# Expert weights in 8 KB runs, with the SSD and routing work in another order, attention scores from high and low parts, and scatters without empty places

## The reference, cut to what matters

```python
h = rms_norm(x, norm_mix)
proj = h @ w_in
# A: attention, 8 heads of 64, causal, with a decay; q and k normalised
sc = einsum('bhqd,bhkd->bhqk', qi, kh) + ci[..., None] - c[:, :, None, :]
# B: GLA, 4 heads, chunks of 64.  C: SSD (Mamba-2), 8 heads, chunks of 64:
y = y_intra + einsum('bhctn,bhcnp->bhctp', cc * exp(acs)[..., None], prev)
y = rms_norm((y + d_skip * xs) * silu(z), out_norm)
x = x + sum(gates * (branches @ w_branch)) @ w_out
t = rms_norm(x, norm_ffn)
# best of 4 groups, then 2 of its 4 experts: 1024 pairs of a token and an expert
for e in range(16):
    hid = silu(t @ w_gate[e]) * (t @ w_up[e])           # 1024 -> 512
    out = out + combine[:, e:e + 1] * (hid @ w_down[e])  # 512 -> 1024
x = x + out
```

## Time and profile before

| | |
|---|---|
| median of three runs | 872.98 us |
| the profiled execution, own time | 872.24 us |
| its span, first to last instruction | 870.5 us |
| mean granted TensorE clock | 0.993 |
| busy: PE, DVE, ACT, POOL | 840.0 (97%), 579.1 (67%), 475.7 (55%), 92.2 us (11%) |
| matmuls on PE | 4188 |
| DMA | 164.26 MB, 189 GB/s over the span |

### The profile page before, as it was taken

One profiled execution on the slowest core, in us unless ns is written; L12 is line 12 of the kernel. 1 busy time (PEld: TensorE's weight loads), 2 busy tenths in 40 slices (PEclk: granted clock), 3 DMA queues, 4 the chain that ended last, 5 costly groups with the idle time before them and its releaser, 6 DMA issues.

```text
span 870.5 us, 11553 instructions
## 1 busy us (share of the span) xinstructions
PE 840.0 (97%) x4188; PEld 673.5 (77%) x4188; DVE 579.1 (67%) x678; ACT 475.7 (55%) x563; POOL 92.2 (11%) x131
## 2 busy tenths in 40 slices
PE   5999999999999989999999999989999999999994
PEld 4777777777877768888888888867888888888883
DVE  5555436766745887324254265788898988889893
ACT  6375445554455242322332332557888788888882
POOL 6510000000000110100000010103112111111001
PEclk9999999999999999999999999999999999999998
DMA  6432012213112031332232494599999999999973
GB/s 213 146 98 72 25 49 98 98 48 98 50 49 97 1 96 49 100 104 97 90 104 97 185 321 164 204 383 347 386 388 369 362 371 377 374 366 352 376 295 49
DMA packets 60173, 164.26 MB, mean 189 GB/s; under 512 B 9592, under 2 KB 10705, under 8 KB 60130
## 3 DMA queue, kind: packets, MB, share of 16 engines
q1 hardware_dynamic: 51504, 145.89, 45.5%
q0 software_dynamic: 4464, 12.66, 6.4%
q10 hardware_dynamic: 4162, 5.13, 1.7%
HBM read 154.16 MB, written 13.11 MB: 192 GB/s over the span
## 4 chain that ended last, share of the span: by engine, by line
PE 90%; DVE 4%; ACT 2%; DMA 1%; issue 1%; POOL 0%; POOLq 0%; DVEq 0%; ACTq 0%
PE bank L1986 26%; PE bank L1988 25%; PE bank L1987 25%; PE bank L2457 1%; PE bank L2108 1%; PE bank L2139 1%; PE bank L2124 1%; DMA xg<-h2rows,tabid 1%; PE bank L2464 1%; PE bank L2096 1%; PE bank L2240 1%; PE bank L2324 1%; PE bank L2190 1%; PE bank L2198 0%; ACT whi L715 0%
## 5 line engine op out<-in xcount | busy, mean ns | idle before, releaser
L737 DVE TENSOR_TENSOR wlo<-mstage,whi 128x2048 fp32r<-128x2048 f32 x95 | 215.5, 2290 | 28.9 <-ACT whi L715 28.8
L715 ACT ACTIVATE whi<-mstage 128x2048 fp32r<-128x2048 f32 x96 | 183.8, 1919 | 25.6 <-PE bank L1988 25.1
L737 DVE TENSOR_TENSOR wlo<-stage,whi 128x2048 fp32r<-128x2048 f32 (+1 forms) x39 | 87.8, 2251 | 96.1 <-ACT whi L715 95.4
L1986 PE MATMUL bank<-hTh,whi 128*128 128x512 f32 x368 | 149.4, 406 | 0.3 <-DVE wlo L1445 0.3
L1988 PE MATMUL bank<-hTh,wlo 128*128 128x512 f32 x368 | 143.7, 390 | 0.0
L1987 PE MATMUL bank<-hTl,whi 128*128 128x512 f32 x368 | 143.4, 390 | 0.0
L715 ACT ACTIVATE whi<-stage 128x2048 fp32r<-128x2048 f32 (+1 forms) x39 | 73.0, 1874 | 75.9 <-PE bank L1988 71.1
L1986 PE MATMUL bank<-whi,xTh 128*128 128x512 f32 (+1 forms) x264 | 104.3, 395 | 2.1 <-DVE xTl L1809 1.1
L1988 PE MATMUL bank<-whi,xTl 128*128 128x512 f32 (+1 forms) x264 | 101.5, 384 | 0.0
L1987 PE MATMUL bank<-wlo,xTh 128*128 128x512 f32 (+1 forms) x264 | 101.2, 383 | 0.0
L1986 PEld LDWEIGHTS bank<-hTh,whi 128*128 128x128 f32 x368 | 69.2, 188 | 17.4 <-issue 2.8
(11 more groups left out here) (383 smaller groups left out, 1333.6 us busy)
## 6 DMA issues: line engine op xcount, KB each, us to landing
mstage<-in_w_exp_gate SPq DMA_DIRECT2D x32, 1024.0 KB, 11.9
mstage<-in_w_exp_up SPq DMA_DIRECT2D x32, 1024.0 KB, 12.0
mstage<-in_w_exp_down SPq DMA_DIRECT2D x32, 1024.0 KB, 12.4
stage<-in_w_in SPq DMA_DIRECT2D x28, 1024.0 KB, 5.0
stage<-in_w_branch SPq DMA_DIRECT2D x6, 1024.0 KB, 5.0
stage<-in_w_out SPq DMA_DIRECT2D x4, 1024.0 KB, 5.1
xin<-in_x SPq DMA_DIRECT2D x4, 512.0 KB, 5.3
x<-in_x SPq DMA_DIRECT2D x4, 512.0 KB, 7.4
```

The costliest lines, as they stand in the source:

```text
L715: nc.scalar.activation(whi_of(u)[:, :, 0:n], source_of(u)[:, :, 0:n], ACT.Copy).then_inc(hi_ready, 1)
L737: nc.vector.tensor_tensor(wlo_of(u)[:, :, 0:n], source_of(u)[:, :, 0:n], whi_of(u)[:, :, 0:n].bitcast(F32), ALU.subtract).then_inc(lo_read ...
L1986: t.matmul(out, lhs[0], rhs[0], start=start, stop=False)
```

## The change

1. **Start.** DVE scales tile 0 too, in the order square 0, scale 0, square 1, scale 1, scale 2, scale 3, and only then copies the parameter columns. PE transposes tile 3 last, after the parameter rows.
2. **Scores.** `foxq` and `foxk` are split into high parts (ACT, 8 copies of 128x512) and low parts (DVE, 8 subtractions). A score is three fp32r matmuls for each head instead of one in float32.
3. **GLA.** One piece of projection is moved ahead of `gout 0`, behind `gprep 1`.
4. **SSD.** DVE updates the state ahead of the output rows, whose work is now an item of its own, `ssdY`. The `lo` items go later.
5. **Routing.** The rows of padding behind the output are gone, and the DMA that cleared them. `normed` makes four operations of 128x256 of every fourth column, instead of two of 128x512 of every second. DVE takes splits of weights and the permutation's low parts in another order. `table()` also makes `tabh`, ids of half rows.
6. **Experts.** Each partition gets one run of 8 KB from a unit of weights, where it got two of 4 KB. So it holds four rows next to each other of gate and up, and two of down; `hid_rows` therefore takes every second column of `hid` as the operand of the transpose. The wait for the load four units before is gone.
7. **Scatters.** Empty places are skipped by a bounds check. The last item has two scatters, each of half rows, which start when their half of `yrow` is there.

```diff
@@ schedule()
-    out += [("gprep", 1), ("gout", 0), ("gmul", 0)]
+    out += [("gprep", 1)]
+    fill(1, last)
+    out += [("gout", 0), ("gmul", 0)]
     lows()
-    fill(5, last)
+    fill(4, last)
...
         out.append(("ssdB", i))
-        lows()
         if i:
             out.append(("ssdC", i - 1))
+        out.append(("ssdY", i))
+        if i == 0:
+            lows()
         fill(3, gates)
         if i + 1 < NT:
             out.append(("ssdA", i + 1))
         out.append(("ssdN", i))
         if i == 0:
             out.append(("gmul", 1))
-        lows()
+        elif low:
+            out.append(low.pop(0))
...
@@ SP, load(u)
-                if not ovf and u >= U_MOE + 4:
-
-                    sp.wait_ge(mstaged[(u - 4 - U_MOE) % 12], after(m, 16, 16 * ((u - 4 - U_MOE) // 12 + 1)))
-                sp.dma_start(mstage[k][:, :, :].rearrange("p (g r) n -> p g (r n)", r=2), src).then_inc(mstaged[k], 16)
+                sp.dma_start(mstage[k][:, :, :].rearrange("p c n -> p (c n)"), src).then_inc(mstaged[k], 16)
...
-                    return w[e, kh * 512:(kh + 1) * 512, :].rearrange("(g p r) n -> p g (r n)", p=P, r=2)
+                    return w[e, kh * 512:(kh + 1) * 512, :].rearrange("(p r) n -> p (r n)", r=4)
...
-                    return w_exp_down[e, fh * 256:(fh + 1) * 256, :].rearrange("(j p) n -> p j n", p=P)
+                    return w_exp_down[e, fh * 256:(fh + 1) * 256, :].rearrange("(p j) n -> p (j n)", j=2)
...
@@ POOL, scatter(i, par)
-                                     compute_op=ALU.add).then_inc(added, 16)
+                                     bounds_check=T - 1, oob_is_err=False, compute_op=ALU.add).then_inc(added, 16)
...
-                scatter(i, i % 2)
+                if i < NEXP - 1:
+                    scatter(i, i % 2)
+            for half in range(2):
+                pool.wait_ge(free[2 + half], B0[2 + half] + NEXP)
+                g.indirect_dma_start(acc.rearrange("t (h c) -> (t h) c", h=2),
+                                     bass.IndirectOffsetOnAxis(tabh[:, half:half + 1], 0),
+                                     yrow[:, 1, half * 512:half * 512 + 512], None, bounds_check=2 * T - 1,
+                                     oob_is_err=False, compute_op=ALU.add).then_inc(added, 16)
...
@@ ACT, start
-            act.wait_ge(rst_done, 1)
-            a.activation(xn[:, 0, :], xin[:, 0, :], ACT.Copy, scale=rst[:, 0:1]).then_inc(xna_done, 1)
...
@@ DVE, normed(i)
-                for r in range(2):
+                for r in range(4):
...
@@ PE, score
-                    for hh, r in enumerate(rows_of):
-                        t.matmul(bank[4 + hh][:, 0:w], foxq[r, pr, i * P:(i + 1) * P], foxk[r, pr, 0:w],
-                                 start=True, stop=False)
+                    for a, b, first in ((foxqh, foxkh, True), (foxqh, foxkl, False), (foxql, foxkh, False)):
+                        for hh, r in enumerate(rows_of):
+                            t.matmul(bank[4 + hh][:, 0:w], a[r, pr, i * P:(i + 1) * P], b[r, pr, 0:w],
+                                     start=first, stop=False)
...
@@ PE, transposes of hid
-                    ins = t.transpose(bank[6][:, j * P:(j + 1) * P], hid[:, j * P:(j + 1) * P], ident[:, :])
+                    ins = t.transpose(bank[6][:, j * P:(j + 1) * P], hid_rows(j), ident[:, :])
```

More of the change, by code:

```diff
@@ L94, in schedule @@
              (0, 1, 3): [("cumh",)], (1, 0, 3): [("tokrows",)], (2, 0, 1): [("bcum",)]}
+    for q in range(4):
+        early.setdefault((1, 1, q), []).append(("parts", q))
     waiting = [[], []]
@@ L137, in schedule @@
         out += exps[1] + taken[half:]
+        if n < 3:
+            out.append(("parts", 5 + n))
         if nxt is not None:
@@ L1083, in _ @@
                     step(a.activation(lge[:, :, :], lge[:, :, :], ACT.Ln, bias=1.0), lnv_done, 2)
+                elif kind == "parts":
+                    m = it[1]
+                    act.wait_ge(qn_done, m + 1)
+                    step(a.activation((foxqh if m < 4 else foxkh)[:, m % 4, :], (foxq if m < 4 else foxk)[:, m % 4, :],
+                                      ACT.Copy), qh_done, m + 1)
                 elif kind == "cumh":
@@ L1663, in _ @@
                     step(v.tensor_tensor(yd, yd, whole(4), ALU.add), free[4], n)
-                    if i:
-                        n = turn(6, ("ye", i)) + 1
-                        dve.wait_ge(full[6], n)
-                        step(v.tensor_tensor(heads(xdt[:, :]), heads(whole(6)), per_head(eacs[:, i, :]), ALU.mult), free[6], n)
-                        step(v.tensor_tensor(yd, yd, xdt[:, :], ALU.add))
-                    step(v.scalar_tensor_tensor(out=yd, in0=yd, scalar=0.5, in1=zs[:, i, :],
-                                                op0=ALU.mult, op1=ALU.mult), sd_y, i + 1)
                     if i == 0:
@@ L1684, in _ @@
                                  *((free[5], n) if q else ()))
+                elif kind == "ssdY":
+                    i = it[1]
+                    yd = ysd[i % 2][:, :]
+                    if i:
+                        n = turn(6, ("ye", i)) + 1
+                        dve.wait_ge(full[6], n)
+                        step(v.tensor_tensor(heads(xdt[:, :]), heads(whole(6)), per_head(eacs[:, i, :]), ALU.mult), free[6], n)
+                        step(v.tensor_tensor(yd, yd, xdt[:, :], ALU.add))
+                    step(v.scalar_tensor_tensor(out=yd, in0=yd, scalar=0.5, in1=zs[:, i, :],
+                                                op0=ALU.mult, op1=ALU.mult), sd_y, i + 1)
                 elif kind == "ssdN":
@@ L1865, in _, with gated @@
                                  pf[:, :, 0, :].unsqueeze(3), ALU.subtract))
-            split_lo(dve, U_MOE + 2)
+            def gated(n, m=None, per=2):
+                dve.wait_ge(full[1], after(m, per, B0[1] + n + 1))
+                dve.wait_ge(free[0], after(m, per, B0[0] + n + 1))
+                v.tensor_tensor(hid[:, :], act1[:, :], whole(1), ALU.mult).then_inc(free[1], 1)
+            split_lo(dve, U_MOE + 4)
+            split_lo(dve, U_MOE + 5)
+            gated(0)
             dve.wait_ge(r_exp, 1)
@@ L1902, in table @@
                 step(v.tensor_copy(tabid[:, :].unsqueeze(2), slots[:, 0:ITEMS, 0:1]), tab_done, 1)
+                for half in range(2):
+                    step(v.tensor_scalar(tabh[:, half:half + 1], slots[:, NEXP - 1, 0:1], 2.0, float(half), ALU.mult,
+                                         ALU.add))
                 step(v.tensor_reduce(tabw[:, :], slots[:, 0:ITEMS, 1:3], AX, ALU.add), tab_done, 2)
```

110 lines of the change are left out of this document (55 added, 55 removed).

## The result

The change makes the kernel slower: 874.77 us (873.88 to 877.12, 14 runs) against 872.89 (871.88 to 873.59, 14 runs), ratio 1.0028, 95% interval 1.0021 to 1.0035. Forecast were 865.0 us and a range to 869.5. The profiled execution has an own time of 873.92 us and a span of 872.2.

A forecast was written before the change was run, and what follows sets the result against it. PE was taken to bound the kernel, with DVE the bound in routing and the DMA engines close behind. The terms summed to -7.6 us on the profiled 872.24, giving 865.0 us on the median, range 861.5 to 869.5.

The forecast's parts named there:

- SSD term: SSD block 1: the state comes earlier, so PE's 3.26 us wait and the clock loss behind it go; -4.4 us.
- Rival (a): SSD: the wait is only exchanged, delayed splits are late for PE, half the term gone; 867.5 us, chance 0.16.
- Clock: SSD: the half clock behind PE's old wait goes, a gain of 1.4 us, between 1.0 and 1.6.
- Scores: Attention scores: three fp32r passes replace a float32 matmul, shorter at wide widths, +0.1 at 128 keys; -1.5 us.
- GLA: GLA: the moved projection piece covers PE's 0.7 us wait for `kendT`; -0.7 us, bounds -1 to 0.
- Start: Start: moving one scaling from ACT to DVE makes one end better, the other worse; 0, between -0.7 and +0.4 us.
- Routing: Routing and expert 0: an earlier first product is lost again to a later table; +0.3 us, bounds -1.4 and +2.5.
- Rival (b): Expert 0: the down product's wait grows from 0.9 to 2.4 us or more, dropping the clock; 866.3 us, chance 0.13.
- Experts: Experts: longer weight runs gain nothing as PE waits for no weights, and strided `hid` loads stay hidden; 0 us.
- Rival (c): Experts: strided loads of `hid` at half speed cost 7 to 9 us, giving 873 us; chance 0.05.
- Rival (d): Experts: transfers become the bound through 8 KB runs or the uncapped queue; 875 us at 5% longer, chance 0.04.
- Tail: After PE's last matmul: two half-row scatters leave a smaller last transfer; -1.3 us, bounds -2.0 and -0.5.

The follow-up runs named there:

- e1: The changed kernel, but ACT takes the squares of the SSD output rows behind the next block's decay exponentials; 869.90 us, ratio 0.9958.
- e2: The kernel before with the SSD order alone changed; 873.16 us, ratio 0.9999.
- e4: The changed kernel with down weights as before, so transposes of `hid` take neighbouring columns; 873.57 us, ratio 1.0006.
- e3: The changed kernel with the start of before (ACT scales tile 0, old order on DVE and PE); 873.53 us, ratio 1.0003.
- e8: The changed kernel with the wait for the load four units before put back on SP; 875.72 us, ratio 1.0037.
- e5: e1 with the last item added to the output by one scatter of whole rows; 870.05 us, ratio 0.9974.
- e9: e1 with DVE computing the places and weights of the pairs earlier, ahead of splits of weights; 867.58 us, ratio 0.9939.
- e10: e9 with the start of before and down weights as before, transposes of `hid` taking neighbouring columns; 863.76 us, ratio 0.9901.
- e11: e1 with DVE writing `hid` spread, so that the columns of a transpose are neighbours; 874.32 us, ratio 1.0014.
- e6: e1 with DVE making the table of expert 0 ahead of a split of weights; 870.58 us, ratio 0.9976.
- e7: The changed kernel with the edits of e1, e3, e4 and e6 together; 867.71 us, ratio 0.9942.

## Why the prediction was wrong

**The step that failed is in the SSD term:** "Nobody but ACT's square of the rows waits for the output rows at once". That is true of who waits and wrong about what it costs. The square is in ACT's queue ahead of the exponentials of the next block, so with PE over 5 us ahead these are what comes too late. I had followed DVE's order through the block, and not ACT's, though the row that I read had ACT fuller than DVE: 3.40 of 3.5 us against 2.91. Forecast were -4.4 us. Measured are -4.1 at the decay matrices (from -1.74 to -5.88), near what was computed, and +5.3 at the products (to -0.63), so +1.1 in all. Before, the same late exponentials cost nothing, since PE came late as well. e1 shows the cause, and e2 that the SSD part alone gives nothing. Rival (a) had an exchanged wait, but for the splits, and with half of the gain left.

A smaller step was off too: the state was to be there 1.1 us before PE wants it. PE's load of the operand of the second L2250, in PEld's timeline of the changed kernel, still waits for it:

```profile
304.81 0.19 PEld L2250 LDWEIGHTS bank<-acsm,acsw 128*128 128x128 f32 x1 [0.41 <-DVE stt L1699]
```

**Clock.** I took 1.4 us for it behind the old wait, 1.27 of them up to the next projection. In e1, with the stretch at full clock, it takes 306.13 - 304.58 = 1.55 us, the value that I had from block 0, so the size was right. The changed kernel gets less of it, 306.83 - 304.81 = 2.02 us at full clock, since its loads wait there for DVE. That the new wait, shorter by a third, would lower the clock for twice as long was not foreseen. It is the larger part of the loss: PE is still 3.5 us ahead when it starts the products, at 314.71, so 2.9 of the 5.3 us go behind the wait. This price isn't fixed. Five traces have the wait of 2.2 us; in four of them the clock is low for about 6.8 us behind it, in e4 for 3.4, and there the stretch takes 15.76 us.

**Scores.** -1.5 forecast, -1.4 measured (from +1.26 to -0.18). From the first score to the last it is 105.11 us against 106.34, so 1.2 of it is theirs, and 0.2 lie ahead of them. A wide score takes 196.61 - 195.48 = 1.13 us, against 1.09 forecast and 1.30 before; one of 128 keys takes 0.60 instead of 0.49, the +0.1 that was put in.

```profile
195.48 0.50 PE L2138 MATMUL bank<-foxkh,foxqh 64*128 64x512 f32 x2
...
196.61 0.28 PE L2145 MATMUL bank<-maskq,identb 128*128 128x128 bf16 x2
```

**GLA.** -0.7 forecast, -1.6 measured up to block 1 of the SSD. The wait, 0.7 us, accounts for half of it. Another 0.3 belongs to the SSD's order, since e2, which has no other change, gains it there too: from the last score to that place it is 109.26 us before, 108.93 in e2 and 107.70 in the changed kernel. Where the rest comes from was not tried.

**Start.** 0 forecast, +1.26 measured in these two traces and 0.9 on average over all, outside of its bounds either way; 1.2 by e3's median. The bound counted DVE's shorter scaling and not that DVE now stands still between the tiles. The square of tile 1 ends 1.8 us later than before, and so does all that hangs on it, down to `hTl`, for which PE waits 1.4 us.

**Routing.** +0.3 forecast, +0.95 measured (from -0.46 to +0.49). Two of the four low parts come earlier, but the wait for `xTl` shrank only from 1.1 to 0.8 us, because the counts come late: DVE gets them at 568.46 instead of 567.70, and waits for ACT both times. Ahead of them in the chain an operation of POOL, on `g`, took 1.20 us instead of 0.22, and the half split now placed there, 566.37 to 567.6 on DVE, runs beside it. That the one slows the other was not tried. The last operation of the table (`ove`) comes at 592.67 instead of 591.42, 1.25 us later, where I had 0.2 to 0.5. Rival (b) was right in its mechanism: the wait of 0.9 has become 2.6, where I had 2.4. The wait for the first gather, forecast at up to 1 us, is gone. In the profiled execution of the changed kernel the clock stays at 1.00 behind the wait of 2.6, but in others, e1, e3, e4 and e8 with a wait of 2.5 or 2.6, it drops to 0.50. That costs e1 2.7 us against e5, which has the same order there and no drop, and e3 and e4 1.6. Such executions are the likely reason for the spread of the changed kernel up to 877.1: its four runs above 876.7 us have a mean granted clock of 0.988 to 0.990, and the two fastest 0.992. At which wait they lost it isn't shown, since only one execution of it has a trace.

**Experts.** 0 forecast, +1.5 measured. Rival (c) happened in small: 0.069 us more for a load, 64 of them, of which 0.02 each reach the path. Rival (d) did not: the transfers got further ahead.

**Tail.** -1.3 forecast, -0.3 in the changed kernel and -0.5 on average. Both parts are off. The second scatter is issued 0.5 us later after ACT's last scaling than the one before was (864.09 - 862.08 against 861.58 - 860.10), where I had 0.2 to 0.3. From that issue to the end it is 8.1 us instead of 8.9, so half of the columns and half of the places take 0.8 us from the transfer, where I had let them take 1.5.

Together, in the two profiled executions: +1.3 for the start, -1.4 scores, -1.6 GLA, +1.1 SSD, +0.2 between the SSD and expert 0, +0.95 routing, +1.5 experts, -0.3 tail, which is the +1.7 of the spans. Of the 9.3 us between that and the forecast of -7.6, 5.5 are the SSD's.

## What to carry to other kernels

When an operation is moved behind another, look on every engine for what waits for the *other* operation, and then at what is queued behind that wait; an engine's queue turns a harmless late result into a late input of something else. A wait's price on PE is its length and the clock behind it, so look at whether it can be kept short, not only at the sum of waits: here 2.6 us often cost another 1.6 to 2.7 us, and 1.3 us cost nothing. And two gains of one kernel don't add if the first brings PE forward into the place where the second engine was late anyway.

## What the runs showed of the hardware

- **Clock behind a wait.** Behind the wait for `dec`, 2.2 us, it fell to 0.50 in all five traces that have it (the changed kernel, e2, e3, e4, e8), for 6.8 us in four and 3.4 in e4. Behind PE's wait ahead of the down product the granted clock stayed at 1.00 for waits of 0.9 (before, e2) and 1.3 us (e9, e10), was at 0.50 in part or all of the next 4 us for 2.5 and 2.6 us in four (e1, e3, e4, e8), stayed at 1.00 for 2.6 us in two (the changed one, e5), and fell for 2.9 and 3.5 us (e11, e6, e7).
- **Steps of 16 bytes.** `normed` in the changed kernel:

```profile
L1781 DVE SCALAR_TENSOR_TENSOR xn<-x,rst,gainb x12: 668/676/694, 518.2 to 547.8; 128x256 f32<-128x256 f32 x12
```

  0.676 us for 256 columns, where 512 took 0.752: 2.7 us a tile instead of 1.5, against the 1.9 that I took. The Trainium skill, SBUF — State Buffer, section Door 1: The DMA port swizzle, had it right with its two accesses to a 16-byte line. The prediction had its cost on the path at nothing or, by that rule, at 0.3 us. It was hidden: the distance between PE's places in the SSD and in expert 0 changes by 0.2 us.
- **Steps of 8 bytes are not free everywhere.** By the same rule they would be. DVE's `normed` of before fits, with 0.752 for 512. PE's load of `hid` doesn't: 0.209 instead of 0.140 us.
- **A write spread over two places** 512 bytes apart, one float to each in turn, made DVE's product of 128x512 take 1.06 us instead of 0.68 (e11).
- **An indirect DMA costs POOL 1.55 us** whether it carries 128 rows of 4 KB or of 2 KB.
